# Compression's two wide projections cut into halves, each around a merge gate, in a one-core Trainium2 model kernel

## The reference, cut to what matters

```python
z = u @ w_in                                   # queries, keys, values, gates, conv, merge gates
zq, zkv, zg, zc, zm = jnp.split(z, IN_SPLITS, axis=-1)

def compress(kv, pos, w1, w2):                 # once for keys, once for values
    blocks = kv[:, :, idx] + pos               # 15 windows of 32 tokens, stride 16
    flat = blocks.reshape(..., n_cmp, CMP_LEN * HEAD_DIM)      # 2048 wide
    return jax.nn.gelu(flat @ w1) @ w2         # w1: 2048 x 256, w2: 256 x 64

c = causal_dwconv(c_val * sigmoid(c_gate), conv_w, conv_b)     # 31 taps, 512 channels
ga, gb = jnp.split(jax.nn.sigmoid(zm), 2, axis=-1)             # 16 merge gates of 128 columns
h = h + (ga * y_a + gb * y_b) @ w_out
```

## Time and profile before

| | us |
|---|---|
| median of 3 runs | 891.61 |
| lowest, highest | 890.43, 893.21 |
| the profiled execution's own time | 891.58 |
| its span in the trace | 889.8 |
| PE busy | 864.0 (97%) |
| POOL busy | 627.0 (70%) |
| DVE busy | 565.7 (64%) |
| ACT busy | 484.0 (54%) |

### The profile page before, as it was taken

The page is one execution under the profiler, slowest core; times in us unless marked ns, Lnnn a source line. Parts: engine busy times, 40 slices in busy tenths (PEclk is TensorE's granted clock), DMA queues, the critical chain, the costliest instruction groups (busy, mean ns, idle before and its releaser), DMA issues.

```text
span 889.8 us, 18240 instructions
## 1 busy us (share of the span) xinstructions
PE 864.0 (97%) x7027; PEld 827.0 (93%) x7027; DVE 565.7 (64%) x1550; ACT 484.0 (54%) x919; POOL 627.0 (70%) x280
## 2 busy tenths in 40 slices
PE   7999999999999999999999999999999999999995
PEld 6999988889998899999999989888999999999994
DVE  5997757773243567677358997765556666641165
ACT  6654465664546456563755467665554444554351
POOL 3899755555997456473979798453777888889680
PEclk9999999999999999999999999999999999999997
DMA  8577633332775343443657576232565666667511
GB/s 318 183 214 218 187 116 96 96 95 51 217 226 152 116 143 105 134 119 96 184 172 213 166 207 205 87 120 71 167 169 173 190 180 186 183 191 220 181 48 48
DMA packets 38534, 138.85 MB, mean 156 GB/s; under 512 B 4272, under 2 KB 4272, under 8 KB 38448
## 3 DMA queue, kind: packets, MB, share of 16 engines
q1 hardware_dynamic: 38448, 137.69, 51.6%
HBM read 136.63 MB, written 1.05 MB: 155 GB/s over the span
## 4 chain that ended last, share of the span: by engine, by line
PE 74%; DVE 5%; POOL 4%; ACT 2%; issue 2%; DVEq 0%; ACTq 0%
PE ps L581 20%; PE ps L582 20%; PE ps L583 20%; POOL wl L533 4%; PE ps L931 2%; PE ps L802 1%; PE ps L626 1%; PE ps L955 1%; PE ps L608 1%; ACT wh L1047 1%; PE ps L826 1%; PE ps L798 1%; PE ps L708 1%; PE ps L775 1%; PE ps L944 1%
## 5 line engine op out<-in xcount | busy, mean ns | idle before, releaser
L533 POOL TENSOR_TENSOR wl<-raw,wh 128x1024 fp32r<-128x1024 f32 x254 | 611.4, 2434 | 221.7 <-ACT wh L1047 221.5
L581 PE MATMUL ps<-uh,wh 128*128 128x256 f32 x1248 | 353.8, 283 | 6.5 <-DVE ul L1544 2.7
L582 PE MATMUL ps<-ul,wh 128*128 128x256 f32 x1248 | 349.3, 280 | 0.0
L583 PE MATMUL ps<-uh,wl 128*128 128x256 f32 x1248 | 348.8, 279 | 0.0
L1047 ACT ACTIVATE wh<-raw 128x1024 fp32r<-128x1024 f32 x256 | 264.6, 1054 | 86.7 <-PE ps L583 83.2
L581 PEld LDWEIGHTS ps<-uh,wh 128*128 128x128 f32 x1248 | 235.0, 188 | 11.8 <-issue 3.3
L582 PEld LDWEIGHTS ps<-ul,wh 128*128 128x128 f32 x1248 | 235.1, 188 | 0.0
L583 PEld LDWEIGHTS ps<-uh,wl 128*128 128x128 f32 x1248 | 234.6, 188 | 0.0
L1702 DVE TENSOR_TENSOR h<-ps,h 128x256 f32<-128x256 f32 x32 | 13.6, 424 | 106.5 <-PE ps L583 106.3
L582 PE MATMUL ps<-ffl,wh 128*128 128x256 f32 x176 | 49.3, 280 | 0.0
L581 PE MATMUL ps<-ffh,wh 128*128 128x256 f32 x176 | 49.1, 279 | 0.0
(11 more groups left out here) (359 smaller groups left out, 1761.1 us busy)
## 6 DMA issues: line engine op xcount, KB each, us to landing
raw<-slabs SPq DMA_DIRECT2D x256, 512.0 KB, 4.0
h<-x_fm SPq DMA_DIRECT2D x4, 256.0 KB, 6.4
out_fm<-outb SPq DMA_DIRECT2D x4, 256.0 KB, 2.2
cst<-shape_consts SPq DMA_DIRECT2D x1, 768.0 KB, 8.8
vec<-vectors SPq DMA_DIRECT2D x1, 303.5 KB, 3.9
pin<-p_fm SPq DMA_DIRECT2D x1, 256.0 KB, 5.5
```

The lines of the kernel that those rows point to most:

```text
L533: nc.gpsimd.tensor_tensor(wl[:, s % PART_RING, :], raw[:, s % RAW_RING, :], wh[:, s % PART_RING, :].bitcast(f32), ALU.subtract).then_inc(s ...
L581: nc.tensor.matmul(res, w_h, a_h, start=first, stop=False)
L582: nc.tensor.matmul(res, w_h, a_l, start=False, stop=False)
L583: ins = nc.tensor.matmul(res, w_l, a_h, start=False, stop=last)
```

## The change

`hk` and `hv` are each cut at k-step 8 into two halves of two slabs. Between `hk`'s halves stands `mg8` (before: ahead of `hk`), between `hv`'s halves stands `mg10` (before: ahead of `hv`). The gates' two transposes move with `mg8`, to just ahead of `hk`'s second half. The stream's slabs are laid out in the same new order; the number of slabs and the jobs' bank numbers stay. DVE makes `cxl` before a piece of twelve convolution steps instead of after it, and its other pieces are resized: from the taking of `gates` to that of `mg11` they were 5, 18, 6, 6 and 21 steps and are 5 and 6, 12, 12, 12 and 9. ACT splits slabs up to five beyond the second half's first slab ahead of each gelu.

```diff
+HID_EARLY = 8
+SPLIT[f"mg{GATES_BEFORE[0]}"] = [("hk", 0, HID_EARLY), (f"mg{GATES_BEFORE[0]}", 0, 8), ("hk", HID_EARLY, 16)]
+SPLIT[f"mg{GATES_BEFORE[2]}"] = [("hv", 0, HID_EARLY), (f"mg{GATES_BEFORE[2]}", 0, 8), ("hv", HID_EARLY, 16)]
...
-            for n in ["kvc0", "kvc1", "nq0", "nq1", "nq2", "nq3", "ks", "kw", "vsw", "gates",
-                      f"mg{GATES_BEFORE[0]}"]:
+            for n in ["kvc0", "kvc1", "nq0", "nq1", "nq2", "nq3", "ks", "kw", "vsw", "gates"]:
                 project(n, u, u_lo)
 
-            wait(pe, "norm_scaled", n_fin1.d0 + KD)
-            wait(pe, "gates_sig", 1)
-            for b in range(TB):
-                ins = nc.tensor.transpose(PS_TR[:, b * P:(b + 1) * P], gT[:, b * P:(b + 1) * P], ident)
-            ins.then_inc(sem("gates_tr"), 1)
-            project("hk", tile_of(cxh), tile_of(cxl), lambda k: pe.wait_ge(sem("cmp_lo"), 1))
-            for n in GATES_BEFORE[1:3]:
-                project(f"mg{n}", u, u_lo)
-            project("hv", tile_of(cxh), tile_of(cxl))
+            def hidden_part(name, gate):
+
+                ready = lambda k: pe.wait_ge(sem("cmp_lo"), 1)
+                project_part(name, tile_of(cxh), tile_of(cxl), 0, HID_EARLY, ready)
+                project(f"mg{gate}", u, u_lo)
+                if name == "hk":
+                    gates_transpose()
+                project_part(name, tile_of(cxh), tile_of(cxl), HID_EARLY, 16, ready)
...
+            hidden_part("hk", GATES_BEFORE[0])
+            project(f"mg{GATES_BEFORE[1]}", u, u_lo)
+            hidden_part("hv", GATES_BEFORE[2])
             project(f"mg{GATES_BEFORE[3]}", u, u_lo)
...
             def hidden(i, s):
+                feed_slabs(jobs[f"h{s}"].at[HID_EARLY] // BLK + PART_RING - 1)
                 o = output(f"h{s}")
...
-            conv31(12)
             dve.wait_ge(sem("cmp_hi"), 1)
             tt(cxl[:], cx[:], cxh[:].bitcast(f32), ALU.subtract).then_inc(sem("cmp_lo"), 1)
+            conv31(12)
             take("gates", gT[:])
             conv31(5)
...
+            conv31(6)
             take_gate(GATES_BEFORE[0])
-            conv31(18)
+            conv31(12)
             for n in GATES_BEFORE[1:3]:
                 take_gate(n)
-                conv31(6)
-            conv31(21)
+                conv31(12)
+            conv31(9)
             take_gate(GATES_BEFORE[3])
```

More of the change, by code:

```diff
@@ L873, in _, with gates_transpose @@
                     norm_spread(n_fin1)
-            for n in ["kvc0", "kvc1", "nq0", "nq1", "nq2", "nq3", "ks", "kw", "vsw", "gates",
-                      f"mg{GATES_BEFORE[0]}"]:
+            for n in ["kvc0", "kvc1", "nq0", "nq1", "nq2", "nq3", "ks", "kw", "vsw", "gates"]:
                 project(n, u, u_lo)
-            wait(pe, "norm_scaled", n_fin1.d0 + KD)
-            wait(pe, "gates_sig", 1)
-            for b in range(TB):
-                ins = nc.tensor.transpose(PS_TR[:, b * P:(b + 1) * P], gT[:, b * P:(b + 1) * P], ident)
-            ins.then_inc(sem("gates_tr"), 1)
-            project("hk", tile_of(cxh), tile_of(cxl), lambda k: pe.wait_ge(sem("cmp_lo"), 1))
-            for n in GATES_BEFORE[1:3]:
-                project(f"mg{n}", u, u_lo)
-            project("hv", tile_of(cxh), tile_of(cxl))
+            def hidden_part(name, gate):
[5 more added lines that the diff above has]
+                project_part(name, tile_of(cxh), tile_of(cxl), HID_EARLY, 16, ready)
+            def gates_transpose():
+                wait(pe, "norm_scaled", n_fin1.d0 + KD)
+                wait(pe, "gates_sig", 1)
+                for b in range(TB):
+                    ins = nc.tensor.transpose(PS_TR[:, b * P:(b + 1) * P], gT[:, b * P:(b + 1) * P], ident)
+                ins.then_inc(sem("gates_tr"), 1)
+            hidden_part("hk", GATES_BEFORE[0])
+            project(f"mg{GATES_BEFORE[1]}", u, u_lo)
+            hidden_part("hv", GATES_BEFORE[2])
             project(f"mg{GATES_BEFORE[3]}", u, u_lo)
@@ L1304, in _ @@
             hidden(0, "k")
-            for n in GATES_BEFORE[1:3]:
-                merge_gate_by_tanh(n)
+            merge_gate_by_tanh(GATES_BEFORE[1])
+            merge_gate_by_tanh(GATES_BEFORE[2])
             hidden(1, "v")
```

## The result

| | median, us | lowest to highest | runs | ratio to the kernel before |
|---|---|---|---|---|
| first comparison: before | 892.18 | 890.43 to 893.21 | 6 | |
| first comparison: after | 896.96 | 895.19 to 898.5, and one of 2154.42 | 6 | 1.0049 [1.0031, 1.0067] |
| second comparison: before | 892.54 | 889.98 to 897.16 | 35 | |
| second comparison: after | 895.28 | 894.48 to 896.84 | 12 | 1.003 [1.0015, 1.0046] |

The change makes the kernel slower: 4.8 us in the first comparison, 2.7 in the second. The forecast was 893.1, 1.5 us slower.

The account below looks back on a forecast made before the run. PE, busy 97% of the span, was taken as the bound, with POOL short over the stretch and DVE's queue setting mg1. 0 (POOL) + 0 (ACT) + 1.5 (DVE) = +1.5 us gave 893.1, range 890.8 to 894.8.

Parts of the forecast that it names:

- PE and POOL, sum 0: Up to mg11: PE's waits only change place, slab 12 is ready at 530.75 in both, mg11 starts at 530.89; 0 us.
- The low part sooner, cost 0: cxl starts at 502.08 instead of 506.90, holds one POOL split 2.06 us as before, earlier; no PE wait for cxl.
- ACT, 0: At hv's first half: hk's gelu comes at about 518, 1.8 us ahead of need; cost 0.
- DVE, +1.5: mg10's late take, 21 steps behind it: mg11's take 1.6 us late, mg1 from 538.53 to 540.1; +1.5 us.
- Its first split at 495.58 lies ahead of everything that changed: Start of POOL's unbroken chain: taken as unmoved by the change, so slab 12 is ready at 530.75 in both.
- 891.58 + 1.5 = 893.1: Whole kernel: the profiled execution of before plus DVE's 1.5 us; that execution stands 0.03 us from the median.
- Everything behind mg1 hangs on that start and moves rigidly: Behind mg1: all that follows shifts with mg1's start, 538.53 to 540.1; the sum stays +1.5 us.
- Rival 3: At mg1 and behind: TensorE's granted clock falls once, 1.5 us more, 894.6 in all; chance 0.08.
- Rival 1: POOL's hold under cxl goes or shrinks, or takes come sooner: no difference, about 891.9; chance 0.18.
- rival 2: At hv: PE's waits simply vanish, 2.6 us gained, 889.0; chance 0.05.

Follow-up runs that it names:

- The two kernels without just the five extra steps: The change with 17 and 16 steps behind mg9's and mg10's takes, not 12 and 21: 894.93 us; with DVE's ogl subtractions also moved: 891.79 us.
- Moving the two subtractions: Kernel before, DVE's two ogl subtractions put behind the last pair's two multiplications: 891.4 us, later 891.25; the change with the same move: 894.02, later 893.03.
- both padded kernels: Kernel before with 14 or 29 matmuls added ahead of mg1: 893.12 us (ratio 1.0021) and 894.84 us (1.004).
- low-part-only kernel: Kernel before with only cxl made twelve convolution steps sooner: 891.89 us, ratio 0.9994.
- the one with DVE's whole order: Kernel before with all of DVE's reordering (cxl sooner, pieces 11, 12, 12, 21) and nothing else: 893.66 us, ratio 1.0002.
- the first of the two tried for speed: Kernel before with the two ogl subtractions moved, ACT splitting two more slabs ahead of its wait for cx: 897.36 us, ratio 1.0052.

## Why the prediction was wrong

- **PE and POOL, sum 0: right.** From the start of POOL's chain slab 12 had no earlier date: mg11 starts at 533.37 - 2.44 = 530.93, forecast 530.9. The wait ahead of mg10 was to be 1.2 us and is 0.71, with 0.26 at hv's second slab and 0.34 at its fourth.
- **The low part sooner, cost 0: right.** It starts at 504.52 - 2.44 = 502.08, as forecast, is ready at 507.32, and PE wants it later. The kernel with this part alone is level with before.
- **ACT, 0: right.** The gelu comes at 519.92 - 2.44 = 517.5, forecast 518, and PE doesn't wait for it.
- **DVE, +1.5: right, 1.44.** Idle before mg10's take 1.86 (forecast 1.9), its take at 529.31 - 2.44 = 526.87 (526.98), mg11's take at 535.44 (535.6), hgl at 537.2 (537.3), mg1 at 539.97 (540.1). The 0.06 us between a take and ACT's tanh were counted as slack and are none (0.04 us here); that changes nothing. The stretch costs 1.42 to 1.44 in three traces and 0 with 16 steps. The two kernels without just the five extra steps show that these steps are the cost.
- **"Its first split at 495.58 lies ahead of everything that changed", and "891.58 + 1.5 = 893.1": this step failed first.** The forecast took one execution of before as the ground, with all its dates ahead of the stretch, and so put what comes ahead of it at 0 without a reason. In the trace of after that split starts at 498.02. Of the 2.44 us, 2.2 come at 406 us, at the meeting (PE's offset goes from -0.06 to 2.12 there), which the edit doesn't touch. Moving the two subtractions takes it away: no run of 24 of the kernel before is above 893 then. A meeting that comes out late on one side of a comparison only is more than the whole forecast.
- **"Everything behind mg1 hangs on that start and moves rigidly": this step failed too.** It holds in the trace of after, where the offset stays near 3.9 us to the end, and in both padded kernels. It does not hold in an execution whose granted clock falls in the stretch behind mg1, +1.5 us there. Rival 3 named the mechanism, the place and the price (1.5), and got 0.08. The argument against it was a stretch of 524 to 532 us with the clock at 1.00 and 6.05 of 8 us busy; the stretch that mattered has 1.88 of 3.20, which the forecast's own two waits implied. What the runs show is 11 such executions of 24, not 8 in 100. With half of the runs at +1.5 and half at +3.0, the fair forecast was about 893.5 to 894, with a range beyond 894.8; without the meeting even that lies 3 us under the first comparison.
- **How the first comparison adds up is an estimate.** By sizes, 896.96 is 891.4 + 1.4 (the late take) + 2.2 (the meeting) + 1.5 (the fall) = 896.5. Its one profiled execution was the one of 2154 us, so no trace shows the three together. In the second comparison the trace has the first two, and its time is 895.29.
- **What stays open.** In the second comparison, 11 of 35 runs of before lie where the meeting puts them (894.98 and above), and by its lowest run (894.48, 2.1 us above the lowest one with the subtractions moved) all twelve of after's do. Up to 406 us its engines have the same work and the split and the first subtraction stand 0.30 or 0.31 us apart in all traces, whichever way the tie comes out; why the changed program should lose it more often was not found, nor whether it does on every chip. So it is not shown either that these 2.2 us have to do with the change.

Rival 1 (no difference) is refuted by the DVE rows and mg1's start, rival 2 (the waits vanish, 889.0) by POOL's unchanged total of 2.0 us.

The best kernel found is the one before with the two subtractions moved: 891.4 and 891.25, ratios 0.9984 [0.9968, 0.9999] and 0.9986 [0.9973, 0.9998]. It takes off the upper tail rather than time from a typical run.

## What to carry to other kernels

When a reorder moves waiting from one engine to another, price what the waiting engine owes next: here 1.9 us of idling in front of one take, with 21 steps behind it, was the whole cost in the stretch, and moving five of those steps paid it back. A forecast for an engine that is 97% busy is not one number once the edit adds waits of 0.7 us to it: give the clock's fall the share of executions that it deserves, and price both levels; here PE waited, the clock fell in some executions and not in others with the same rows. And before reading a difference of 2 us, look at all runs of the kernel before: if they fall in two groups, find what splits them and take it away in both kernels. Last, when a trace is late as a whole, count from the engine that sets the pace (here the start of POOL's chain): that turned costs of 0 to 0.3 us of scatter into figures that repeat within 0.1.

## What was not expected of the hardware

- A tie closer than the trace's hundredths of a microsecond decides whether a subtraction on DVE takes 0.4 us or 2.6 (0.75 or 2.97 us for the two), 100 us away from any edit. The same second subtraction stands 2.6 us in at least five earlier pairs of heads in the traces of before and after alike, so the meeting at 406 us is the exception in that it can come out either way.
- Eight small additions with operands in SBUF (128 x 120) took 6.50 us where POOL stood idle for part of the time, and 10.7 us beside POOL's unbroken splits.
- The granted clock also fell at the last norm, near 852 us, in three of sixteen traces (the low-part-only kernel, the one with DVE's whole order, and the first of the two tried for speed), and not in those of before or after, at about 1.5 us of loss each. The kernel with DVE's order and the kernel before have the same busy time of PE ahead of it, 1.68 of 3.00 us, and only one falls. With DVE's order:

```profile
849.00:852.00 3.00, 1.68 (x12) 1.47 (x13) 2.06 (x15) 2.72 (x3) 3.00 (x2) 0.96 0.03 5
852.00:855.50 3.50, 3.50 (x20) 3.50 (x19) 2.15 (x4) 1.37 (x2) 3.50 (x2) 0.54 0.75 208
```

and the kernel before:

```profile
849.00:852.00 3.00, 1.68 (x13) 1.47 (x13) 2.06 (x15) 2.79 (x3) 3.00 (x2) 1.00 0.00 0
852.00:855.50 3.50, 3.50 (x32) 3.50 (x31) 2.45 (x4) 1.37 (x2) 3.50 (x2) 1.00 0.70 198
```
